# Feed-forward block: one more unit of gates and three units of values computed with seven products

## What is computed

```
n2 = rms(h) * w                                    # 514 tokens x 1024
up = causal_depthwise_conv(n2 @ w_up, 3 taps)      # 1024 -> 2 x 2816
gate, val = split(up)
h = h + (silu(gate) * val) @ w_down                # 2816 -> 1024
```

## Time and profile before

| what | value |
|---|---|
| device time, median of 3 runs | 1817.21 us (1817.13 to 1819.65) |
| the profiled execution's own time | 1818.72 us |
| its span in the profile | 1816.9 us |
| granted TensorE clock, mean | 0.998 |
| TensorE matmul busy | 1798.6 us (99%) |
| VectorE busy | 1374.2 us (76%) |
| ScalarE busy | 954.2 us (53%) |
| GpSimd busy | 143.9 us (8%) |

### The profile page before, as it was taken

The page is one execution under the profiler, slowest core; times in us unless marked ns, Lnnn a source line. Parts: engine busy times, 40 slices in busy tenths (PEclk is TensorE's granted clock), DMA queues, the critical chain, the costliest instruction groups (busy, mean ns, idle before and its releaser), DMA issues.

```text
span 1816.9 us, 33004 instructions
## 1 busy us (share of the span) xinstructions
PE 1798.6 (99%) x13702; PEld 1716.0 (94%) x13702; DVE 1374.2 (76%) x2408; ACT 954.2 (53%) x1854; POOL 143.9 (8%) x122
## 2 busy tenths in 40 slices
PE   9999999999999999999999999999999999999998
PEld 8999999978899989999899999999899999999987
DVE  5888897678756777757889797978358888787844
ACT  6222333568734445535556665666347566666632
POOL 0000000000000001010002121111000112111000
PEclk9999999999999999999999999999999999999999
DMA  5222222200222155354347777775332677777431
GB/s 197 94 84 80 93 94 71 94 24 26 70 76 91 61 155 128 91 138 102 110 116 153 156 158 152 161 152 132 117 93 76 130 158 154 158 151 160 113 122 70
DMA packets 239107, 207.19 MB, mean 114 GB/s; under 512 B 6262, under 2 KB 235439, under 8 KB 238958
## 3 DMA queue, kind: packets, MB, share of 16 engines
q1 hardware_dynamic: 180862, 176.24, 31.5%
q0 software_dynamic: 58080, 28.84, 12.9%
q10 hardware_dynamic: 16, 0.00, 0.0%
HBM read 202.97 MB, written 2.10 MB: 113 GB/s over the span
## 4 chain that ended last, share of the span: by engine, by line
PE 90%; DVE 4%; ACT 4%; issue 1%; DMA 0%; DVEq 0%; SPq 0%; ACTq 0%
PE ps L195 60%; PE ps L199 29%; PE ps L204 2%; ACT p L207 1%; DVE wlo L210 1%; DVE ast L1133 1%; ACT whi L207 1%; DVE mxl L210 0%; DMA xt<-in_x_dram 0%; ACT nhi L207 0%; ACT pa L207 0%; ACT at L207 0%; ACT ps L207 0%; DVE na L210 0%; DVE pa L210 0%
## 5 line engine op out<-in xcount | busy, mean ns | idle before, releaser
L210 DVE TENSOR_TENSOR wlo<-raw,whi 128x1024 fp32r<-128x1024 f32 (+1 forms) x355 | 430.0, 1216 | 219.9 <-ACT whi L207 218.4
L207 ACT ACTIVATE whi<-raw 128x1024 fp32r<-128x1024 f32 (+1 forms) x355 | 371.5, 1050 | 240.2 <-PE ps L195 195.4
L195 PE MATMUL ps<-nhi,whi 128*128 128x256 f32 (+3 forms) x1648 | 367.3, 289 | 2.6 <-DVE clo L210 0.8
L195 PE MATMUL ps<-nhi,wlo 128*128 128x256 f32 (+3 forms) x1648 | 363.5, 287 | 0.0
L195 PE MATMUL ps<-nlo,whi 128*128 128x256 f32 (+2 forms) x1520 | 326.4, 287 | 0.0
L195 PEld LDWEIGHTS ps<-nhi,whi 128*128 128x128 f32 x1648 | 266.4, 189 | 6.7 <-DVE clo L210 1.0
L195 PEld LDWEIGHTS ps<-nhi,wlo 128*128 128x128 f32 x1648 | 265.6, 189 | 2.1
L195 PEld LDWEIGHTS ps<-nlo,whi 128*128 128x128 f32 x1520 | 241.1, 189 | 1.9
L199 PE MATMUL ps<-thi,whi 128*128 128x256 f32 x784 | 224.8, 287 | 1.4 <-DVE wlo L210 0.8
L199 PE MATMUL ps<-thi,wlo 128*128 128x256 f32 x784 | 221.6, 283 | 0.0
L199 PE MATMUL ps<-tlo,whi 128*128 128x256 f32 x784 | 221.4, 282 | 0.0
(11 more groups left out here) (342 smaller groups left out, 3391.7 us busy)
## 6 DMA issues: line engine op xcount, KB each, us to landing
raw<-in_w_in_dram SPq DMA_DIRECT2D x90, 1024.0 KB, 5.8
raw<-in_w_up_dram SPq DMA_DIRECT2D x22, 1024.0 KB, 5.1
raw<-in_w_out_dram SPq DMA_DIRECT2D x20, 1024.0 KB, 5.0
s1t<-in_w_in_dram SPq DMA_DIRECT2D x49, 256.0 KB, 3.4
s1t<-in_w_in_dram POOLq DMA_DIRECT2D x49, 256.0 KB, 7.0
raw<-in_w_in_dram POOLq DMA_DIRECT2D x49, 256.0 KB, 4.7
raw<-in_w_down_dram SPq DMA_DIRECT2D x16, 512.0 KB, 3.4
raw<-in_w_conv_out_dram SPq DMA_DIRECT2D x4, 1024.0 KB, 5.0
```

The costliest lines, as they stand in the source:

```text
L195: return pe.put(after, lambda e: e.matmul(o, w, m, start=start, stop=stop_), mark)
L207: return ac.put(after, lambda e: e.activation(o, i, func, **kw))
L210: return dv.put(after, lambda e: e.tensor_tensor(o, a, b, op))
```

## The change

The gates of j = 4 go by seven too, and so do the values of j = 5, 7 and 9. The values' seven uses banks 5, 2 and 3, of which 2 and 3 are pair 1 of the plain tiles. `up_seven` gets its banks as an argument.

```diff
@@ -292,12 +292,12 @@
         SEVEN_AT = [0, 4, 1, 2]
         GROUPS = [(0, 4), (4, 8), (8, 11)]
         DOWN = [(0, 0), (1, 0), (0, 1), (1, 1), (2, 0), (2, 1), (3, 0), (3, 1)]
-        GATES_BY_SEVEN = range(5, 11)
+        GATES_BY_SEVEN, VALUES_BY_SEVEN = range(4, 11), (5, 7, 9)
         first_ffn = len(plan)
         for a, b in GROUPS:
             for j in range(a, b):
                 unit(cols(w_up[0], 256 * j), BY_K if j == 0 else SEVEN if j in GATES_BY_SEVEN else BY_COL)
-                unit(cols(w_up[0], FF + 256 * j), BY_COL)
+                unit(cols(w_up[0], FF + 256 * j), SEVEN if j in VALUES_BY_SEVEN else BY_COL)
             n = b - a
             for j, i in DOWN:
                 unit(cols(w_down[0], 256 * j, 2 * a + n * i, n), [(0, n, 0, 256)])
@@ -1467,7 +1467,7 @@
-            def up_seven(j, atok, jl):
+            def up_seven(j, atok, jl, banks):
 
                 ns = [next_y(), next_y()]
 
@@ -1476,7 +1476,7 @@
-                t = seven([ZR[n] for n in ns], [6, 7, 4], [zr_used[n] for n in ns], hook,
+                t = seven([ZR[n] for n in ns], banks, [zr_used[n] for n in ns], hook,
@@ -1633,12 +1633,14 @@
                     elif j in GATES_BY_SEVEN:
-                        up_seven(2 * j, atok, 2 * (j - ja))
+                        up_seven(2 * j, atok, 2 * (j - ja), [6, 7, 4])
                     else:
                         for c in range(2):
                             z = tile(TQ, NHI, NLO, ntok)
                             up_out(*z, 2 * j + c, atok, 2 * (j - ja) + c)
-                    for c in range(2):
+                    if j in VALUES_BY_SEVEN:
+                        up_seven(NFF + 2 * j, atok, 2 * (j - ja), [5, 2, 3])
+                    for c in range(2) if j not in VALUES_BY_SEVEN else ():
                         v = tile(TQ, NHI, NLO, ntok)
```

## The result

| | before | after |
|---|---|---|
| median of 16 runs | 1818.26 us | 1821.71 us |
| range of the runs | 1816.9 to 1820.99 us | 1820.01 to 1824.27 us |
| profiled execution | 1818.72 us | 1821.72 us |
| its span | 1816.9 us | 1819.8 us |

The ratio is 1.0019, with a 95% interval of 1.0011 to 1.0027: 3.5 us slower, where 2.8 slower was forecast. It is just inside the 0.2% within which I would have called it no change. With 16 runs on either side the interval leaves out 1, so the kernel did get slower. In microseconds the forecast was 1820.0 and 1821.7 was measured; of the 1.7 between them 1.0 is that the forecast started from 1817.2, the median of three runs of the kernel before, and 16 runs give 1818.3.

A forecast was written before the change was run, and what follows sets the result against it. TensorE, busy for 99% of the span, bounds the kernel. 5.4 saved - 3.9 (s1) - 0.5 (banks, j = 8) - 3.8 (first sums) = 2.8 us slower: 1820.0 us, forecast as no change, range 1815.5 to 1825.0.

The forecast's parts named there:

- The waits at the start of group 1: Gates of j = 4: VectorE waits for the first sum, bank 6 is freed late, first product at 669.7: 3.8 us lost.
- The late end of the range: First sum of j = 4 lands at 665.3; group 1 starts 8.0 us late, total 1824.2; late-sum rival's chance 0.14.
- 3.7 + 0.1 = 3.8 us: Start of group 1: first product of the gates of j = 4 at 669.7 instead of 666.02.
- The waits for s1: Third products in gates of j = 5, 6, 10 and values of j = 5, 7, 9 wait for copy s1: 3.9 us.
- Cost at nothing for VectorE's load: In j = 5, 7 and 9 VectorE is over its time by 1.3 us; neighbours cover it, total cost nothing.
- The rival by VectorE's load: VectorE becomes the bound in j = 5, 7 and 9: 6.7 us slower, 1823.9; chance 0.12.
- The rival that the gap does not come: Start of group 1: sum landed in time or bank free, j = 4 costs 0.5: +0.5 us, 1816.7; chance 0.18.
- the rule of the Trainium skill: POOL's first sums for j = 4: by it the landing would tend to the late end; no row shows whether it applies.
- the expected 21.8 us a j: VectorE's work with both units of a j by seven, 17.2 + 4.6, against 20.5 us of TensorE.

The follow-up runs named there:

- The filled gap: Changed kernel plus 30 unread matmuls of 256 columns ahead of the gates of j = 4: 1819.39 us, ratio 1.0006 to the kernel before.
- moving two operations: Changed kernel, but where seven follows seven the first unit's two operations on y come behind s1 of the second: 1820.22 us, ratio 1.0015.
- all seven values: Kernel with changed banks, early first sums and moved operations on y, plus values of j = 4 to 10 by seven: 1807.96 us, ratio 0.9945.
- other banks: Changed kernel, but the first gates by seven of a group use banks 2, 3, 4 in place of 6, 7, 4: 1816.86 us, ratio 0.9992.
- earlier sums: Changed kernel, but the first two sums into S1T are asked for four units earlier: 1816.55 us against 1818.07, ratio 0.9991.
- all values, no remedies: Changed kernel, but the values of j = 4 to 10 all go by seven: 1820.88 us, ratio 1.0017.
- gates of j = 4 alone: Kernel before, with only the gates of j = 4 added to the units by seven, all values plain: 1823.59 us against 1818.10, ratio 1.0030.
- shorter gap: Changed kernel, but last tiles are added to H ahead of the third slot's low part at a group's end: 1820.04 us against 1817.91, ratio 1.0012.
- three remedies: Changed kernel with banks 2, 3, 4 first, first two sums four units earlier, operations on y behind the next s1: 1813.27 us against 1818.07, ratio 0.9974.
- values of j = 10: Kernel with changed banks, early first sums and moved operations on y, plus the values of j = 10 by seven: 1811.85 us against 1817.91, ratio 0.9969.

## Why the prediction was right, and where not

- **The waits at the start of group 1** came as worked out. The first sum was expected on VectorE at 661.2 and started at 661.09, the first product was expected 3.7 us late and was 3.7 late. That it takes both the bank and the late sum is shown by two kernels that each take one away and each give back about 5 us. The late end of the range (a landing at 665.3) did not come up; in one run the sum was 1.5 us later and the gap 4.9.
- **A term was missing.** "3.7 + 0.1 = 3.8 us" was the price of the gap in idle time alone. The clock falls to half behind it, which cost 1.5 us more in the changed kernel's trace and up to 2.7 in others. The filled gap shows that this is due to the idle time.
- **The waits for s1 were mis-sized**: 3.9 us forecast, 2.7 measured. The place and the cause were right, since moving two operations removed these gaps wherever a unit by seven follows another. But a unit of values lost 0.51 us, not 0.69: `s1` starts 2.83 us behind the end of the gates, not 2.95, and the restart costs less than the 0.11 that I added. The gates of j = 6 lost 21.41 - 20.16 - 0.51 = 0.7 us, where I had 1.1.
- These two errors nearly cancel (+1.5 and -1.2), so by luck the sum was closer than its terms.
- **Cost at nothing for VectorE's load**: right. With three values the neighbours cover it, and no product waits for weights in j = 5 to 10. The rival by VectorE's load is false here, and with all seven values it costs 0.5 us a unit at the end of a group, not what I priced it at.
- **The rival that the gap does not come** is what one obtains by design, with other banks or earlier sums. They are 1.2 and 1.5 us faster than before, where the rival had 0.5: the waits for s1 were too dear in it as well. That their times (1816.9 and 1816.6) lie on its 1816.7 is partly luck, for it started from a median of 1817.2.
- Of the rule of the Trainium skill (SBUF — State Buffer, 🔬 SBUF: two separate sides) that VectorE in a 2-port performance mode keeps GpSimd from writing descriptors nothing was seen: POOL issued the first two additions in 2.75 us, as in the earlier trace rows, with VectorE busy for 1.2 of them (the low part at 656.33), and the sum landed as estimated without the rule. No row says in which mode VectorE's work ran, so the rule is neither borne out nor refuted.

## What to carry to other kernels

On a kernel bound by TensorE, see that the first unit of a group finds its inputs and its banks ready before you count on fewer matmuls: here four units saved 5.4 us, and one late start took 5.3. Look for the one transfer that the engine behind it waits for in order, and for what else stands in that engine's list: here a transfer that nobody had missed before held the freeing of a bank three steps further on. Price an idle stretch of TensorE of some 3 us and more at over its length, for in all five traces with one the clock behind it fell; and where two blocks of work follow each other, look which engine's list puts the finishing steps of the first ahead of the first step that the second waits for.

## What the runs showed that I had not expected

A gap of 2.8 to 4.9 us on TensorE at the start of group 1 was followed in each of the five traces that have it by matmuls at 1.2 GHz. The gates of j = 4 then took 11.83, 11.84, 12.67, 12.90 (all values, no remedies) and 13.04 us, for 10.32 behind a short gap: a loss of 1.5 us in two traces and of 2.4 to 2.7 in three. It did not grow with the gap: 13.04 came behind 3.49 us of idle matmul time and 11.84 behind 3.55. The gaps of 0.2 to 0.9 us elsewhere between 640 and 870 us lowered no granted clock. Thirty matmuls that nobody needs made the kernel 2.3 us faster.

But a long gap is not the only way to lose the clock. Between 364 and 370 us, far ahead of the change, TensorE has two gaps of 0.56 and 0.83 us that are the same in every kernel. Behind them the clock fell to half for a time near 373 us in seven of the 13 traces (before, changed, gates of j = 4 alone, early sums, shorter gap, three remedies, values of j = 10) and not in the six others. The windows view of the kernel before, and of the one with other banks:

```profile
374.00:380.00 6.00, 5.00 (x29) 3.36 (x25) 4.29 (x12) 2.88 (x11) 0.00 (x0) 0.79 0.00 0
```
```profile
374.00:380.00 6.00, 5.00 (x39) 3.83 (x36) 5.28 (x13) 4.04 (x15) 0.00 (x0) 1.00 0.00 0
```

From 367.35 to the first matmul of v it is 12.04 us in the first and 10.50 in the second, 1.5 us that no edit made. Two single executions can differ by this much, so compare totals by medians, and traces within the stretch that a change touches. What decides whether the clock falls there is open.

And how much VectorE can take was underrated by adding up single durations: for the seven instructions that a unit by seven adds, 0.08 us of overlap each is 0.6 us, which turns most of the expected 21.8 us a j into the measured 21.1.
